# Which rows of w_down a partition holds in the expert loop of a decoder layer

## The reference

```python
logits = (xt @ w_router + b_router)            # 256 tokens, 32 experts
top_val, top_idx = lax.top_k(logits, 4)
gates = jax.nn.softmax(top_val, axis=-1)
...
def expert_block(args):                        # rows of tokens of one expert
    xb, e = args
    h = xb @ w_gate_up[e] + b_gate_up[e]       # 1024 -> 2048
    g, u = h[:, :D_EXPERT], h[:, D_EXPERT:]
    g = jnp.minimum(g, SWIGLU_LIMIT)
    u = jnp.clip(u, -SWIGLU_LIMIT, SWIGLU_LIMIT)
    glu = g * jax.nn.sigmoid(g * SWIGLU_ALPHA)
    return ((u + 1.0) * glu) @ w_down[e] + b_down[e]    # 1024 -> 1024
```

## Time and profile before

| | |
|---|---|
| median of three runs | 1291.85 us (1291.73 to 1291.88) |
| the profiled execution, its own time | 1291.88 us |
| its span from first to last instruction | 1290.1 us |
| TensorE busy | 1200.7 us, 93% |
| weight loads of TensorE (beside its matmuls) | 522.0 us, 40% |
| VectorE, ScalarE, GpSimd busy | 247.6, 153.3, 56.9 us |
| moved by DMA | 445.33 MB, 345 GB/s over the span |
| share of the SyncE queue's packets in the 16 DMA engines' time | 83.8% |

### The profile page before, as it was taken

How to read it: one execution, slowest core, us unless ns; L and a number is a source line. 1 busy time by engine, 2 the same in 40 slices (tenths; PEclk the granted TensorE clock), 3 DMA queues, 4 the chain that set the end, 5 groups by cost and what they waited for, 6 DMA issues and landing times.

```text
span 1290.1 us, 13406 instructions
## 1 busy us (share of the span) xinstructions
PE 1200.7 (93%) x5074; PEld 522.0 (40%) x5074; DVE 247.6 (19%) x587; ACT 153.3 (12%) x325; POOL 56.9 (4%) x60
## 2 busy tenths in 40 slices
PE   8999999996999999999999999999989999999995
PEld 6686745853333333333333333333333333333332
DVE  2122312115111111112111111112211111111114
ACT  2022221212100101011110101010110101010102
POOL 0011212212000000000000000000000000000000
PEclk9999999997999999999999999999999999999998
DMA  9942233355669999999999999999999999999993
GB/s 357 319 160 78 89 140 131 122 217 195 261 233 410 421 422 420 422 422 422 421 422 422 422 422 422 421 422 422 422 422 422 421 422 423 421 422 422 422 422 128
DMA packets 81846, 445.33 MB, mean 345 GB/s; under 512 B 13144, under 2 KB 14304, under 8 KB 32640
## 3 DMA queue, kind: packets, MB, share of 16 engines
q1 hardware_dynamic: 79808, 440.43, 83.8%
q10 hardware_dynamic: 2016, 4.60, 1.1%
HBM read 443.94 MB, written 1.06 MB: 345 GB/s over the span
## 4 chain that ended last, share of the span: by engine, by line
PE 73%; DMA 16%; ACT 3%; DVE 2%; SPq 2%; issue 2%; POOL 0%; DVEq 0%; ACTq 0%
PE bank L1357 26%; DMA ring<-in_w_gate_up 16%; PE bank L1381 14%; PE bank L1066 9%; PE bank L1079 9%; PE bank L1284 5%; PE bank L1346 3%; SPq L422 2%; PE bank L1333 2%; PE bank L1368 1%; ACT NCt L702 1%; ACT reg_k L675 1%; PE bank L1292 1%; PE bank L1231 1%; PE bank L1166 0%
## 5 line engine op out<-in xcount | busy, mean ns | idle before, releaser
L1357 PE MATMUL bank<-ring,PT 128*64 128x512 f32 x2008 | 441.8, 593 | 9.0 <-DMA ring<-in_w_gate_up 8.7
L1357 PEld LDWEIGHTS bank<-ring,PT 128*64 128x64 f32 x2008 | 141.3, 137 | 304.0 <-issue 265.0
L1381 PE MATMUL bank<-ring,NCt 128*64 128x512 f32 x1024 | 232.0, 600 | 23.5 <-ACT NCt L702 23.5
L1381 PEld LDWEIGHTS bank<-ring,NCt 128*64 128x64 f32 x1024 | 72.9, 137 | 149.9 <-issue 120.0
L976 DVE TENSOR_SCALAR reg_k<-bank 128x512 f32<-128x512 f32 x32 | 22.1, 692 | 470.4 <-PE bank L1357 470.4
L692 ACT ACTIVATE reg_v<-reg_k 128x512 f32<-128x512 f32 x32 | 20.1, 630 | 693.3 <-DVE reg_k L976 693.3
L1066 PE MATMUL bank<-reg_b,ring 128*128 128x256 f32 x384 | 84.6, 380 | 1.8 <-ACT reg_b L630 1.8
L994 DVE COPY vc<-bank 64x512 f32<-64x512 f32 x32 | 21.9, 684 | 317.0 <-PE bank L1381 317.0
L1066 PEld LDWEIGHTS bank<-reg_b,ring 128*128 128x128 f32 x384 | 72.5, 190 | 12.7 <-issue 3.1
L1284 PE MATMUL bank<-reg_a,L 128*128 128x512 f32 x136 | 64.9, 621 | 1.3 <-DVE L L919 1.3
L1333 PE MATMUL bank<-vc,L 128*128 128x512 f32 x128 | 59.2, 605 | 1.6 <-DVE vc L995 1.6
(11 more groups left out here) (198 smaller groups left out, 700.0 us busy)
## 6 DMA issues: line engine op xcount, KB each, us to landing
ring<-in_w_gate_up SPq DMA_DIRECT2D x251, 1024.0 KB, 23.3
ring<-in_w_down SPq DMA_DIRECT2D x128, 1024.0 KB, 21.9
ring<-in_w_in SPq DMA_DIRECT2D x6, 2048.0 KB, 15.2
ring<-in_w_ck SPq DMA_DIRECT2D x2, 2048.0 KB, 20.0
ring<-in_w_cv SPq DMA_DIRECT2D x2, 2048.0 KB, 9.8
ring<-in_w_mix_out SPq DMA_DIRECT2D x2, 2048.0 KB, 7.9
ring<-in_w_cq SPq DMA_DIRECT2D x2, 2048.0 KB, 7.8
ring<-in_w_co SPq DMA_DIRECT2D x2, 2048.0 KB, 9.9
```

The costliest lines, as they stand in the source:

```text
L1357: last = mm(ps[half * CAP:(half + 1) * CAP, :], xgT[:, k, i * CAP:(i + 1) * CAP], w[:, c:c + HALF], start=False, stop=(k == KD - 1))
L1381: last = mm(xy_ps[half * CAP:(half + 1) * CAP, :], hT[:, a:a + CAP], w[:, j, half * HALF:(half + 1) * HALF], start=(k == 0), stop=(k == KD ...
```

## The change

In `chunk_source` the source of the down chunks is read with the two indices in the other order: partition p gets rows p and 128 + p of the chunk's 256, in place of 2p and 2p + 1. The destination in the slot stays: half j behind half 0. In `transpose_h` the four transposes take four blocks of 128 neighbouring columns of `hbuf`, in place of every second column. `down` is unchanged: step k now stands for features 128 * (k % 4) to 128 * (k % 4) + 127 of a half, and the half j of chunk 8 + k // 2 holds just these rows.

```diff
@@ -367,7 +367,7 @@
                 w = w_gate_up[0][bass.ds(e, 1), c * P:(c + 1) * P, :]
                 return w.rearrange("o p n -> (o p) n")
             w = w_down[0][bass.ds(e, 1), (c - GUC) * 2 * P:(c - GUC + 1) * 2 * P, :]
-            return w.rearrange("o (p j) n -> p (o j) n", p=P)
+            return w.rearrange("o (j p) n -> p (o j) n", p=P)
 
@@ -1364,8 +1364,7 @@
             def transpose_h(n1):
                 pe.wait_ge(h_ready, n1)
                 for j in range(4):
-                    c = (j // 2) * 2 * P + j % 2
-                    last = nc.tensor.transpose(tr_ps[:, j * P:(j + 1) * P], hbuf[:, c:c + 2 * P - 1:2], ident)
+                    last = nc.tensor.transpose(tr_ps[:, j * P:(j + 1) * P], hbuf[:, j * P:(j + 1) * P], ident)
                 last.then_inc(hT_done, 1)
```

## The result

The changed kernel takes 1299.23 us (median of four runs, 1299.07 to 1300.62), the kernel before 1291.79 (1291.16 to 1291.88): ratio 1.0062, 95% interval [1.0047, 1.0077]. It is slower, by 0.6%, and the interval leaves no room for "no change".

A forecast was written before the change was run, and what follows sets the result against it. The saturated DMA queue was taken to bound the kernel from its last dry moment to the last gate/up landing, followed by a tail. 1291.88 + 9.1 (down chunks) - 0.2 (transposes) = 1300.8 us; 8-in-10 range 1295.8 to 1304.8.

The forecast's parts named there:

- The bound, and the sum over all chunks from the dry moment on: Expert loop: DMA queue, last dry at 384 to 386 us, sets the end; every later chunk's extra cost adds up.
- rival 2: Expert loop: only the 56 down chunks after 838 us count, 4.4 us, giving 1296.1 us; chance 0.04.
- 116 chunks at 0.078 us: Down chunks on the path, from the dry moment to the last gate/up landing: +9.1 us in all.
- the middle one: Down-chunk packets: line through 8 KiB and w_in's 2 KiB packets; two 4 KiB packets cost 9.8 ns more, +9.1 us.
- The `mem` row: Load of `mem` in 4 KiB pieces, about 18 to 21 us: 160.8 ns a packet, 11.0 ns more for two, 10.2 us.
- the line through w_mix_out: Down-chunk packets: line through 8 KiB and w_mix_out's 2 KiB packets at 81.5 ns; 5.2 ns more for two, 4.8 us.
- SyncE at nothing: Issuing of down chunks: longer waits in an issue delay only the next issue, behind a deep queue; costed at nothing.
- The transposes: Four transposes of h per expert, reading neighbouring columns: 0.18 us less per expert, only the tail's counting, -0.2 us.
- 31 of the 32 count for nothing: Transpose groups of h before the last chunk wait: PE only waits for the chunk longer, so they gain nothing.
- rival 4: Down-chunk loads: the two memory places disturb each other, rate falls to 376 GB/s, +35 us, 1326.7 us; chance 0.05.
- 1 (hidden fixed part): Down-chunk packets: the fixed part is hidden for 4 KiB too, rate stays 422 GB/s, 1291.7 us; chance 0.08.
- 3 (faster): Down-chunk loads: shorter pieces are read at 429 GB/s, -4.8 us, giving 1286.9 us; chance 0.04.

The follow-up runs named there:

- The experiment on experts 2 to 15: Kernel before, with only the down chunks of experts 2 to 15 (56 chunks) loaded from the new source, transposes as before: 1295.38 us, ratio 1.0027.
- the swapped kernel: Kernel before, with each partition's two neighbouring w_down rows put in the slot in swapped order, so 4 KiB packets from neighbouring rows: 1299.88 us, ratio 1.0074.
- 2 KiB: Changed kernel with each 4 KiB row of a down chunk cut into two packets of 2 KiB: 1317.33 us, ratio 1.0201 against the kernel before.
- the two with 16 KiB: Kernel before with 16 KiB down packets, 1288.88 us; the same plus gate/up chunks 0 with 1 and 2 with 3 in 16 KiB packets, 1283.23 us.
- the kernel with pieces 8 KiB apart: Against the kernel before, down chunks take rows 4p and 4p + 2, or 4p + 1 and 4p + 3, transposes every fourth column: 1302.28 us, ratio 1.008.
- the 16 KiB run: Kernel before with four neighbouring w_down rows per partition, one 2 MiB DMA for two slots, transposes of every fourth column: 1288.88 us, ratio 0.9979.

## Why the prediction was right

- **The bound, and the sum over all chunks from the dry moment on**: right. The experiment on experts 2 to 15 shows it apart (4.48 us in the stretch for 56 chunks, 4.3 expected), and with it rival 2 falls.
- **116 chunks at 0.078 us**: measured 0.076, +8.80 us on the path where 9.1 was forecast. Of the three ways to the price of a packet the middle one was nearest: 9.8 ns forecast, 9.7 measured from the pairs. That I took the middle one was a choice, and that it fits to a tenth of a nanosecond is in part luck: the rows before could not decide between w_in's 85.0 ns and w_mix_out's 81.5. The `mem` row's 11.0 was too high; it comes from a stretch of three microseconds with rounded bytes, which I take for the reason; the line through w_mix_out (5.2 ns) was clearly too low. 2 KiB packets in the saturated queue of the expert loop cost 84.9 ns, what the slow 2 KiB rows of w_in say (85.0), not what w_mix_out's 81.5 ns say, which stem from a load of 2 MiB that has the queue to itself. That this is the reason is not shown. What a packet's fixed part consists of, and on which side of the transfer it arises, no run shows either. The Trainium skill ("DMA: Bandwidth & Descriptors", section "iDMA fabric — 4 AXI ports for 8 engines, asymmetric across TPBs") has 408.7 GB/s for a load stream with 4 KiB rows, by my estimate from it 0.081 us more a chunk; the runs' 0.076 is near it.
- **SyncE at nothing**: right, though its issues grew more than I had thought, to 4.47 us, and entered the chain.
- **The transposes**: the mechanism was right, the size was not. I took 0.18 us for a group of four, the difference between L1368 and L1292 in the chain, but it got only 0.09 shorter (0.76 to 0.67). The timelines show why: from the first start to the last end four of L1292 take 0.65 us before and four of L1367 0.66 after (1268.89 to 1269.54, 1271.54 to 1272.20), so the two are alike. But the neighbours of the four of L1292 overlap them at both ends, and the chain gives them only the 0.58 that is left. Four of L1368 take 0.74 in that view, 0.09 more. One group in the tail: -0.1 us, not -0.2.
- **"31 of the 32 count for nothing"** is a little wrong: two groups of them stand in the chain ahead of the dry moment (0.76 us each at 351.18 and 381.16 before, 0.67 each at 350.75 and 380.64 after) and so move it earlier, by 0.09 us each. The run with the transposes alone can't tell this from its noise.
- **The time**: 1300.8 forecast, 1299.23 and 1300.13 measured; +8.9 us against the kernel before forecast, +7.44 and +9.43 measured. The two sets of runs differ by more than the terms that I still argue about. The tail was forecast at 32.9 us and is 33.0 (1298.2 - 1265.24).
- **Two readings that were off**, neither with weight in the sum: the thirteenth slice moves 410 GB/s, and the 420 to 423 begin with the fourteenth. And against rival 4 I took all the mixer's weights for pieces 512 KiB apart. That holds for w_mix_out (402 GB/s); the rows of w_in, with 387 GB/s, have 3,080 numbers, so its pieces lie 1,540 KiB apart.
- **Rivals**: 1 (hidden fixed part) is out by the 60.25 us; 3 (faster) by the 418 GB/s; 4 (distant places) by the 418 GB/s too, and by the swapped kernel, which loses as much a pair without any distance.

## What to carry to other kernels

On a queue that never runs dry, count packets, not only bytes: here each one more cost about 9.5 ns on its engine, from 2 KiB to 16 KiB. Four differences of the table give 9.5 to 9.7 (changed, 2 KiB and the two with 16 KiB, over 116 x 8, 116 x 24, 116 x 4 and 232 x 4 packets, small ones not counted), the neighbours and experts 2 to 15 give 10.0; only the kernel with pieces 8 KiB apart gives more, 12.1, by its slow start. All of it went into the stretch, also where TensorE seemed to set the pace. When a layout can be chosen freely, as the order of summed features can, give a partition neighbouring rows in one piece as long as possible, and let the transposes (0.09 us dearer in a group of four) take the strided columns. Measure such a cost between the last dry moment of the queue and the last landing waited for: for the changed kernel, its repetition and the half of it with the source alone it gave 880.75, 880.62 and 880.69 us, where the times of one kernel spread over 3 us. But it is one execution for each kernel: set it beside the times, as the 16 KiB run shows, where the stretch gained 4.5 us and the median time 3.1.

## What I had not expected of the hardware

- A DMA packet can hold 16 KiB, and what a packet less gains from 8 to 16 KiB (4.51 us over 464, 9.7 ns, or 8.6 with the small packets counted) is about what it gains from 4 to 8 KiB (8.80 us over 928, 9.5 ns).
- Weight loads from every second and every fourth column took about the same in the median (209 and 213 ns; neighbouring columns 141).
- With more packets per chunk SyncE's queue takes fewer chunks ahead: from issue to landing the chunks on the chain took 25.99 us before, 24.65 with 4 KiB and 24.0 with 2 KiB down packets, but 27.5 with 16 KiB.
